# A two-layer mixer and MoE block: the first layer's experts with whole 128-column weight blocks, a looped TensorE program and a wider row selection

## What is computed

```python
def ec_moe(h, w_router, w_e_gate, w_e_up, w_e_down):
    b, t, d = h.shape
    cap = EC_CAPACITY * t // N_EXPERTS          # 64 latents, 32 context rows per expert
    aff = jax.nn.softmax((h @ w_router).astype(jnp.float32), axis=-1)
    vals, idx = lax.top_k(jnp.swapaxes(aff, 1, 2), cap)
    xs = jax.vmap(lambda hb, ib: hb[ib])(h, idx)
    hid = jax.nn.silu(jnp.einsum('becd,edf->becf', xs, w_e_gate)) * jnp.einsum('becd,edf->becf', xs, w_e_up)
    ys = jnp.einsum('becf,efd->becd', hid, w_e_down) * vals[..., None].astype(h.dtype)
    return jax.vmap(lambda yb, ib: jnp.zeros((t, d), yb.dtype).at[ib.reshape(-1)].add(yb.reshape(-1, d)))(ys, idx)
```

## Time and profile before

| | |
|---|---|
| median of 3 runs | 3610.44 us (3601.64 to 3614.49) |
| profiled execution: span from first to last instruction | 3608.9 us |
| profiled execution: its own time apart from the span | not given |
| stage of the first layer's experts, first to last weight matmul | 1193.31 to 1999.41 us, 806.10 us |
| TensorE busy over the span | 93% |

### The profile page before, as it was taken

How to read it: one execution, slowest core, us unless ns; L and a number is a source line. 1 busy time by engine, 2 the same in 40 slices (tenths; PEclk the granted TensorE clock), 3 DMA queues, 4 the chain that set the end, 5 groups by cost and what they waited for, 6 DMA issues and landing times.

```text
span 3608.9 us, 71927 instructions
## 1 busy us (share of the span) xinstructions
PE 3372.9 (93%) x30572; PEld 2302.5 (64%) x30572; DVE 1174.2 (33%) x2567; ACT 707.2 (20%) x1346; POOL 116.6 (3%) x191
## 2 busy tenths in 40 slices
PE   7899999999999899999999989899999999999998
PEld 4456757678764776777677656667677564444544
DVE  1443415346625111111111453425274332222222
ACT  3313321122322000000001432320132201111111
POOL 0000100000000000000000000100000000000000
PEclk9999999999999999999999999999999999999999
DMA  5511120021035899999999401120212269999996
GB/s 226 227 47 59 34 82 13 30 71 46 14 128 220 344 358 352 356 366 373 353 364 365 167 12 62 52 82 13 87 39 76 109 267 416 416 417 419 416 414 289
DMA packets 101983, 738.34 MB, mean 205 GB/s; under 512 B 8272, under 2 KB 14672, under 8 KB 59744
## 3 DMA queue, kind: packets, MB, share of 16 engines
q1 hardware_dynamic: 90512, 692.54, 48.7%
q0 software_dynamic: 11216, 42.00, 4.0%
HBM read 710.34 MB, written 18.92 MB: 202 GB/s over the span
## 4 chain that ended last, share of the span: by engine, by line
PE 73%; DMA 14%; DVE 7%; issue 3%; ACT 3%; DVEq 0%; POOL 0%; SPq 0%; ACTq 0%; POOLq 0%
PE psum L664 14%; PE psum L1265 9%; PE psum L1256 8%; DMA ring<-in_w_e_gate 8%; PE psum L554 8%; PE psum L547 5%; PE psum L1297 5%; PE psum L1117 4%; PE psum L666 3%; DMA ring<-in_w_ada 2%; PE psum L1303 2%; DMA ring<-in_w_e_down 2%; PE psum L531 2%; PE psum L1313 2%; DVE work L2013 2%
## 5 line engine op out<-in xcount | busy, mean ns | idle before, releaser
L664 PE MATMUL psum<-HT,ring 128*128 128x256 f32 x2560 | 599.7, 388 | 13.4 <-DVEq L2266 5.3
L664 PEld LDWEIGHTS psum<-HT,ring 128*128 128x128 f32 x2560 | 488.0, 194 | 98.1 <-issue 21.6
L1265 PE MATMUL psum<-work,ring 128*64 128x96 f32 x11264 | 485.9, 247 | 43.4 <-issue 32.2
L1265 PEld LDWEIGHTS psum<-work,ring 128*64 128x64 f32 x11264 | 471.5, 137 | 59.9 <-issue 49.5
L1496 ACT ACTIVATE work<-psum,small 128x768 f32<-128x768 f32 (+4 forms) x208 | 146.1, 703 | 696.7 <-PE psum L1303 325.6
L554 PE MATMUL psum<-ring,HT 128*128 128x512 f32 (+1 forms) x768 | 276.0, 521 | 0.0
L1256 PE MATMUL psum<-ring,work 128*64 128x256 f32 x1024 | 243.9, 393 | 29.1 <-DMA ring<-in_w_e_gate 28.2
L1257 PE MATMUL psum<-ring,work 128*64 128x256 f32 (+1 forms) x1024 | 238.0, 372 | 0.0
L1499 ACT ACTIVATE work<-psum 128x256 f32<-128x256 f32 (+7 forms) x219 | 103.5, 473 | 652.8 <-PE psum L554 237.8
L1297 PE MATMUL psum<-ring,work 128*64 128x512 f32 x960 | 220.3, 598 | 9.9 <-DMA ring<-in_w_e_down 9.9
L554 PEld LDWEIGHTS psum<-ring,HT 128*128 128x128 f32 x768 | 145.8, 190 | 127.3 <-issue 120.5
(11 more groups left out here) (243 smaller groups left out, 3805.9 us busy)
## 6 DMA issues: line engine op xcount, KB each, us to landing
ring<-in_w_e_gate SPq DMA_DIRECT2D x64, 2048.0 KB, 11.8
ring<-in_w_e_up SPq DMA_DIRECT2D x48, 2048.0 KB, 12.7
ring<-in_w_e_down SPq DMA_DIRECT2D x48, 2048.0 KB, 10.6
ring<-in_w_ada SPq DMA_DIRECT2D x24, 2048.0 KB, 12.4
ring<-in_w_e_up SPq DMA_DIRECT2D x32, 1536.0 KB, 10.2
ring<-in_w_gate SPq DMA_DIRECT2D x16, 2048.0 KB, 8.1
HT<-in_w_e_up SPq DMA_DIRECT2D x16, 2048.0 KB, 23.0
ring<-in_w_e_gate SPq DMA_DIRECT2D x16, 1536.0 KB
```

The source lines that it names most:

```text
L664: pe.matmul(b[:, 0:256], w[:, k, d4 * P:(d4 + 1) * P], HT[:, k, off:off + 256], start=(k == 0), stop=(k == KD - 1))
L1265: ins = pe.matmul(b[lo:lo + 64, f * cap:(f + 1) * cap], w[:, k, c0:c0 + 64], e_xs[:, k, 0:cap], start=(k == 0), stop=(k == KD - 1))
```

## The change

There are four edits, all in the first layer's experts:

- `gate_up` computes a block of 128 hidden columns with one weight block of 128 columns and not two of 64; the output covers all 128 PSUM partitions at once.
- `e_sel` is 128 columns wide for each token tile: the selection of 64 latent rows stands there twice, that of 32 context rows four times. `choose` then needs one `matmul` for each token tile. The clearing of `e_sel` goes, since every column is written.
- TensorE's program for the first 15 experts is a loop in the first layer too; the last expert stays written out.
- `e_ta` and `e_rows` move behind the wider `e_sel`.

```diff
-        e_sel = xr[:, 0:NT * CAPS].rearrange("p (t j) -> p t j", t=NT)
+        e_sel = xr[:, 0:NT * P].rearrange("p (t j) -> p t j", t=NT)
...
                     for t in () if two else range(CT, NT):
-                        for lo in (0, 64):
-                            ins = pe.matmul(banks[5][lo:lo + CAP_L, 0:2], e_sel[:, t, 0:CAP_L], e_ta[:, t, :],
-                                            start=(t == CT), stop=(t == NT - 1))
+                        pe.matmul(banks[5][:, 0:2], e_sel[:, t, :], e_ta[:, t, :], start=(t == CT), stop=(t == NT - 1))
                     for t in range(0 if two else CT):
-                        for q in range(4):
-                            ins = pe.matmul(banks[5][32 * q:32 * q + CAP_C, 2:4], e_sel[:, t, CAP_L:CAPS], e_ta[:, t, :],
-                                            start=(t == 0), stop=(t == CT - 1))
+                        ins = pe.matmul(banks[5][:, 2:4], e_sel[:, t, :], e_ta[:, t, :], start=(t == 0), stop=(t == CT - 1))
...
                                 for k in range(KD):
-                                    for half in range(2):
-                                        lo, c0 = 64 * half, f * P + 64 * half
-                                        ins = pe.matmul(b[lo:lo + 64, f * cap:(f + 1) * cap], w[:, k, c0:c0 + 64], e_xs[:, k, 0:cap],
-                                                        start=(k == 0), stop=(k == KD - 1))
+                                    ins = pe.matmul(b[:, f * cap:(f + 1) * cap], w[:, k, f * P:(f + 1) * P], e_xs[:, k, 0:cap],
+                                                    start=(k == 0), stop=(k == KD - 1))
...
-                if two:
-                    with pe.Fori(0, NE - 1) as e:
-                        c.begin(e, per)
-                        expert(e, False)
-                        c.e = None
-                    c.finish_loop(NE - 1)
-                else:
-                    for e in range(NE - 1):
-                        expert(e, False)
+                per = {"xs": 1, "sel": 1, "idx_next": 1, "rows_in": 16, "ys_a": 1, "hid_f": 3}
+                per |= {"hid": 3, "f_free": 4, "sel_kept": 1} if two else {"ys_d": 1}
+                with pe.Fori(0, NE - 1) as e:
+                    c.begin(e, per)
+                    expert(e, False)
+                    c.e = None
+                c.finish_loop(NE - 1)
...
-                if L == 0:
-                    S(dve.memset(e_sel, 0.0))
...
-                        w0, cp = (0, CAP_L) if off else (CAP_L, CAP_C)
-                        tt(e_sel[:, a:b, w0:w0 + cp], cc("iota")[:, 0:cp].unsqueeze(1).to_broadcast([P, b - a, cp]),
-                           s_pc[:, 0, a:b].unsqueeze(2).to_broadcast([P, b - a, cp]), ALU.is_equal)
+                        cp = CAP_L if off else CAP_C
+                        of = [P, b - a, P // cp, cp]
+                        tt(e_sel[:, a:b, :].rearrange("p t (i j) -> p t i j", j=cp), cc("iota")[:, 0:cp].unsqueeze(1).unsqueeze(1).to_broadcast(of),
+                           s_pc[:, 0, a:b].unsqueeze(2).unsqueeze(3).to_broadcast(of), ALU.is_equal)
```

More of the change, by code:

```diff
@@ L434, in hybrid_layers @@
         e_affT, e_wk, e_mk, e_cu = (xr[:, i * T:(i + 1) * T] for i in range(4))
-        e_sel = xr[:, 0:NT * CAPS].rearrange("p (t j) -> p t j", t=NT)
-        e_ta = xr[:, NT * CAPS:NT * (CAPS + 2)].rearrange("p (t c) -> p t c", t=NT)
-        e_rows = xr[:, NT * (CAPS + 2):NT * (CAPS + 2) + D]
+        e_sel = xr[:, 0:NT * P].rearrange("p (t j) -> p t j", t=NT)
+        e_ta = xr[:, NT * P:NT * (P + 2)].rearrange("p (t c) -> p t c", t=NT)
+        e_rows = xr[:, NT * (P + 2):NT * (P + 2) + D]
         e_hid = xr[:, 4 * T:4 * T + FF]
@@ L1426, in moe @@
                 pe.wait_ge(sems["idx_next"], c.nth("idx_next"))
-                per = {"xs": 1, "sel": 1, "idx_next": 1, "rows_in": 16, "ys_a": 1, "hid_f": 3, "hid": 3, "f_free": 4, "sel_kept": 1}
-                if two:
-                    with pe.Fori(0, NE - 1) as e:
-                        c.begin(e, per)
-                        expert(e, False)
-                        c.e = None
-                    c.finish_loop(NE - 1)
-                else:
-                    for e in range(NE - 1):
-                        expert(e, False)
+                per = {"xs": 1, "sel": 1, "idx_next": 1, "rows_in": 16, "ys_a": 1, "hid_f": 3}
[5 more added lines that the diff above has]
+                c.finish_loop(NE - 1)
                 expert(NE - 1, True)
```

## The result

The changed kernel takes 3711.74 us (median of 4 runs, 3707.40 to 3714.11). The kernel before, run beside it, takes 3608.89 us (3601.64 to 3614.49). The ratio is 1.0273, with an interval from 1.0251 to 1.0295: the change costs 103 us, and the time lies far above the range that I gave.

The account below looks back on a forecast made before the run. TensorE and the DMA engines were both taken as near their end. PE's 30 + 1.5 us, partly taken back by weights, left 22: 3610.4 - 22 = 3588 us, own range 3580 to 3598, 8 in 10 3569 to 3610.

Parts of the forecast that it names:

- What bounds the kernel: First layer's experts: TensorE and DMA engines both near their end; 32.2 us of PE's "issue" waits are instruction fetches.
- Whole blocks at 0: Gate and up: 352 whole-block MATMULs an expert at 82 ns, as pairs of halves cost; 0 change in array time.
- My own sign of being wrong: In the changed kernel's profile, MATMULs starting 0.1 us or more apart would show the prediction wrong.
- loads of whole blocks not hidden: Rival in gate and up: 320 us if all loads are exposed, 160 us if each call's first, giving 3748 us; chance 0.08.
- The upper end of the term: Whole blocks in gate and up: at most 0.06 us more for each load that isn't hidden.
- The loop: TensorE's first 15 experts: a resident body of about 1010 instructions loses its fetches, 30 us off PE; back edge 0.
- the rule of the Trainium skill: Instructions prefetched in blocks of 256; a branch outside two held blocks forces a fetch; refetched-loop rival, 3605 to 3615 us, 0.06.
- Where the stall goes: First layer's experts: late weights take back part of PE's about 32 us; 22 us kept.
- the 48.0 that I took for the DMA engines alone: Expert period in us if DMA alone bounds it, from expert 13's 367 GB/s at 0.97 busy; 50.4 before the change.
- all of PE's gain is kept: Rival for the first layer's experts: loads land earlier without fetches, 32 us gained, 3578 us, down to 3572; chance 0.17.
- the 32 us that I called the most PE could give: PE's side of the sum: 30 us from the loop and 1.5 us from `choose`.
- `choose` and `select`: `choose` 0.1 us an expert less, 1.5 us in all; wider `select` on VectorE hidden, 0.

## Why the prediction was wrong

**What bounds the kernel: right.** The 32 us of "issue" were instruction fetches: in the hinted loop with halves, where the body is kept, they fall to 4.8. The changed kernel has no issue row any more either, but that proves nothing, since the whole blocks alone take it away. That TensorE and the DMA engines were near their ends together was right as well.

**Whole blocks at 0: the step that failed.** I took a `matmul` with 128 weight columns at 82 ns, from the nearest row in shape, the transposes of the earlier trace rows, and 82 ns there and for a pair of halves looked like agreement. Measured are 112 ns. The agreement said nothing of loads: both rows have 96 moving columns. The timeline of the kernel before shows it in rows with other numbers of them:

```profile
3063.27 0.71 PE L1224 MATMUL psum<-const,X 64*128 64x64 f32 x8
2029.81 1.04 PE L580 MATMUL psum<-const,X 128*128 128x128 f32 x8
2030.69 7.07 PE L547 MATMUL psum<-HT,ring 128*128 128x256 f32 x32
1176.48 0.63 PE L642 MATMUL psum<-const,work 128*64 128x2 f32 x16
```

Transposes with 128 weight columns step at 61 to 63 ns with 64 moving columns (the first line, second layer, all but the first step), and at 109 or 110 with 128 (the second). MATMULs with 256 moving columns step at 216 (the third: 7.07 less 0.38 us over 31 steps). A pair of halves with 2 moving columns takes 58 or 59 (the fourth, all but one pair). So 109 / 128 and 216 / 256 both give about 0.85 ns a moving column, and 96 of them come to some 81 ns, an estimate: my 82 ns was the time of the moving columns in both places, and neither row could show what the load of a `matmul` with 128 columns costs.

The trace of before had a row of the right kind: L1166, 32 MATMULs of a `matmul` with 128 weight columns and 128 moving ones in 3.90 us, which is 3.90 less 0.28 over 31, or 117 ns a step, 111 or 112 in all but two. Its steps alone would not have settled it, since 128 moving columns take 109 ns in the transposes. The lengths of its loads were the sign. Timeline of the kernel before, and the groups of its weight loads (last number ahead of the second bar: mean ns):

```profile
1959.48 3.90 PE L1166 MATMUL psum<-work,const 128*128 128x128 f32 x32
```

```profile
L1224 PEld LDWEIGHTS psum<-const,X 96*128 96x128 f32 x123 | 10.8, 141 | 2.1 <-issue 0.3
...
L1166 PEld LDWEIGHTS psum<-work,const 128*128 128x128 f32 x32 | 3.7, 192 | 0.1
```

A load of L1166 lasts 192 ns, against 141 for the transposes and 137 for halves, and I read the MATMULs only. At 112 ns the sum would have been 5632 x 0.0293 = 165 us on gate and up, less at most 52 us of waits: some 3723 us, against the 3712 measured. My own sign of being wrong, MATMULs 0.1 us or more apart, is what the trace of after shows.

**The rival that came** is the last one, loads of whole blocks not hidden, which I gave 0.08. Its direction was right, its mechanism half. It expected 57 ns at each first load of a call, 160 us; in fact every load costs 29 ns over the pair of halves, 165 us. That the two sums are so near is chance. The upper end of the term, 0.06 us a load, did hold the truth; my range of 8 in 10 left that case out, because I read the five steps at 82 ns as evidence against it.

**The loop: the mechanism right, the place of its gain wrong.** The body of the changed kernel is 1023 recorded instructions, about as counted, and no packet comes in a turn. But its 30 us could not be had here: the whole blocks alone took every issue wait away. And for halves, where there was something to gain, the plain loop loses some 127 us. Of the rule of the Trainium skill ("Runtime: NRT & Kernel Launch", section "Instruction fetch mechanics") the runs bear out a part. Its two blocks of 256 are not TensorE's limit, since 1023 and 1415 were kept; its 2048 instructions are not passed by the 1768 that the hinted loop keeps; its warning of a fetch at a taken branch is what the plain loop of 1767 shows.

**Where the stall goes: wrong for the kernel as changed, near for the hinted one.** I expected the weights to take back a part, at 49 us an expert and some 375 GB/s. In the changed kernel PE is the later one everywhere, and waits for weights fell to 1.9 us. With halves and the hint the rate is 376 GB/s as forecast, but waits for weights don't grow (15.9 us), and an expert in the loop takes 47.4 us in the mean (46.3 to 48.4), below the 48.0 that I took for the DMA engines alone: a bound drawn from 0.97 of them busy at 367 GB/s, 378 at 1.00, was too tight, for here 0.98 of them carry 376, which is 384 at 1.00. What makes the few per cent, the runs don't show. That kernel's 3574 us is the rival "all of PE's gain is kept", which I put at 3578. Its gain of 38 us is more than the 32 us that I called the most PE could give: the 7.3 us of busy time above weren't in my sum.

**`choose` and `select`.** `choose` went from 1.04 to 1.29 us, not to 0.98: its loads too are of 128 columns, 112 ns each. Four microseconds in all, and unseen alone. `select` is hidden, as argued: the two edits by themselves gave 0.9994.

## What to carry to other kernels

Cost a matmul by the longer of two paces: that of its moving columns, and that of its weight loads. Take the second from a row with the same kind of instruction, the same number of weight columns and so few moving columns that they don't set the step themselves. A transpose is another kind, and the lengths of the loads in the weight-load rows tell them apart. Two rows that agree may agree because of something else that they share. Ask whether an instruction wait is hidden by another part of the change before counting its end as a gain, and run the parts alone: here the part that looked free cost 94 us and left nothing for the loop to save. A loop in place of a long written-out program is worth trying with a hint for its back edge; the instruction packets in a turn tell whether the body is kept.

## What the runs showed of the hardware that I had not expected

- A load of 128 weight columns for an f32 `matmul` paces TensorE at 112 ns, with 2 or 96 moving columns (and with 128, where the moving columns alone take 109). A `transpose` with 128 weight columns steps at 61 to 63 ns with 64 moving columns, 82 or 83 with 96 and 109 or 110 with 128. A pair of 64-column loads for the two halves of the array, in turns, steps at 58 or 59 with 2 moving columns and at 82 or 83 with 96. Why the load of a transpose is the shorter one, no run here shows.
- A loop body on TensorE of 1023 or 1415 recorded instructions is kept; bodies of 1575 to 1767 are fetched anew at each turn, nine packets of 16 KB, with two waits of some 5.4 us. With a hint for the back edge a body of 1768 is kept. Why the limit without the hint lies so low stays open. That the code behind the branch is fetched and pushes the head out would fit the nine packets, since one expert's written-out code is 6.9; no run here shows what the packets held.
